# Hi and lo halves of activation tiles interleaved word by word, so that stationary operands have a step of two

## What is computed

```python
# first block: pooling and windowed attention branches, then
ff = square(relu(h2 @ w_up)) @ w_down                 # w_up 1024 x 4096
x = x + rmsnorm(ff)
# second block, layer 0, for latent and for context rows
b_gate, c_gate, u = split(h @ w_in, 3)
y = conv1d_depthwise_3(c_gate * u) + conv_b
h = h + g1 * ((b_gate * y) @ w_out)
h = h + g2 * ((silu(m @ w_gate) * (m @ w_up)) @ w_down)   # hidden 2816
# layer 1: attention whose q and kv come from low-rank latents
q = rms_norm(q_lat) @ w_q_up          # latent 768
kv = rms_norm(kv_lat) @ w_kv_up       # latent 256, keys of both row sets
# then softmax attention, output product, and the same feed-forward (latent rows only)
```

## Time and profile before

| | us |
|---|---|
| median of 3 runs | 1435.29 |
| lowest and highest | 1434.83, 1439.27 |
| the profiled execution | 1439.03 |
| its span, first to last instruction | 1437.2 |

### The profile page before, as it was taken

One profiled execution on the slowest core, in us unless ns is written; L12 is line 12 of the kernel. 1 busy time (PEld: TensorE's weight loads), 2 busy tenths in 40 slices (PEclk: granted clock), 3 DMA queues, 4 the chain that ended last, 5 costly groups with the idle time before them and its releaser, 6 DMA issues.

```text
span 1437.2 us, 17619 instructions
## 1 busy us (share of the span) xinstructions
PE 1342.5 (93%) x7376; PEld 1116.1 (78%) x7376; DVE 803.8 (56%) x1087; ACT 544.6 (38%) x679; POOL 3.5 (0%) x10
## 2 busy tenths in 40 slices
PE   5999779999999999999999999998789988799998
PEld 4877678899777788877777777887667766699997
DVE  5666565458664455662525252537556664656666
ACT  5353343454431123422121212125455552544432
POOL 0000000000000000000000000000000000000000
PEclk9999979999999999999999999999889998899999
DMA  8536436545644532363535353412121311345441
GB/s 307 192 117 251 174 110 249 213 176 180 230 154 197 205 117 88 135 245 127 226 124 227 124 227 125 150 43 92 33 87 48 117 59 59 117 159 194 175 175 59
DMA packets 23782, 218.80 MB, mean 152 GB/s; under 512 B 3104, under 2 KB 8224, under 8 KB 10656
## 3 DMA queue, kind: packets, MB, share of 16 engines
q1 hardware_dynamic: 21328, 209.67, 40.2%
q10 hardware_dynamic: 1520, 4.98, 0.9%
q0 software_dynamic: 864, 3.15, 0.7%
HBM read 216.74 MB, written 1.05 MB: 152 GB/s over the span
## 4 chain that ended last, share of the span: by engine, by line
PE 77%; DVE 12%; ACT 7%; issue 3%; DMA 1%; ACTq 0%; DVEq 0%
PE bank L454 23%; PE bank L455 22%; PE bank L456 22%; DVE w_lo L1432 4%; PE turned L471 3%; PE mod_ps L492 3%; ACT w_hi L980 2%; DVE scaled L1473 2%; PE bank L861 2%; PE small L867 2%; DVE gated L1778 1%; DMA raw<-in_w_branch 1%; ACT xn L987 1%; PE small L511 1%; DMA raw<-in_w_out 1%
## 5 line engine op out<-in xcount | busy, mean ns | idle before, releaser
L454 PE MATMUL bank<-act_hi,w_hi 128*128 128x256 f32 (+1 forms) x1208 | 399.7, 331 | 8.8 <-DVE act_lo L1457 6.3
L455 PE MATMUL bank<-act_lo,w_hi 128*128 128x256 f32 (+1 forms) x1208 | 395.8, 328 | 0.0
L456 PE MATMUL bank<-act_hi,w_lo 128*128 128x256 f32 (+1 forms) x1208 | 395.5, 327 | 0.0
L1432 DVE TENSOR_TENSOR w_lo<-raw,w_hi 128x2048 fp32r<-128x2048 f32 (+4 forms) x168 | 338.2, 2055 | 89.8 <-ACT w_hi L980 89.7
L980 ACT ACTIVATE w_hi<-raw 128x2048 fp32r<-128x2048 f32 (+4 forms) x168 | 280.1, 1715 | 210.0 <-PE bank L456 169.7
L454 PEld LDWEIGHTS bank<-act_hi,w_hi 128*128 128x128 f32 x1208 | 231.8, 192 | 42.8 <-issue 17.0
L455 PEld LDWEIGHTS bank<-act_lo,w_hi 128*128 128x128 f32 x1208 | 232.0, 192 | 19.5 <-issue 0.7
L456 PEld LDWEIGHTS bank<-act_hi,w_lo 128*128 128x128 f32 x1208 | 231.8, 192 | 19.3
L454 PE MATMUL bank<-w_hi,h_hi 128*128 128x512 f32 x392 | 155.4, 396 | 4.0 <-DVE h_lo L1830 2.3
L455 PE MATMUL bank<-w_lo,h_hi 128*128 128x512 f32 x392 | 153.4, 391 | 0.0
L456 PE MATMUL bank<-w_hi,h_lo 128*128 128x512 f32 x392 | 153.3, 391 | 0.0
(11 more groups left out here) (227 smaller groups left out, 1421.5 us busy)
## 6 DMA issues: line engine op xcount, KB each, us to landing
raw<-in_ffn SPq DMA_DIRECT2D x35, 2048.0 KB, 8.1
raw<-in_mlp SPq DMA_DIRECT2D x24, 2048.0 KB, 8.0
raw<-in_mod_gate SPq DMA_DIRECT2D x7, 2048.0 KB, 8.1
raw<-in_conv_in SPq DMA_DIRECT2D x8, 1536.0 KB, 7.1
raw<-in_w_gates SPq DMA_DIRECT2D x4, 2048.0 KB, 8.5
raw<-in_w_branch SPq DMA_DIRECT2D x4, 2048.0 KB, 7.9
raw<-in_mla_q SPq DMA_DIRECT2D x4, 1152.0 KB, 5.3
raw<-in_w_in SPq DMA_DIRECT2D x2, 2048.0 KB, 14.0
```

The lines of the kernel that those rows point to most:

```text
L454: te.matmul(dst, sh, mh, start=(j == 0), stop=False)
L455: te.matmul(dst, sh, ml, start=False, stop=False)
L456: last = te.matmul(dst, sl, mh, start=False, stop=(j == len(terms) - 1))
L1432: ve.tensor_tensor(w_lo[:, s, part], raw[:, at % 2, part], w_hi[:, s, part].bitcast(f32), ALU.subtract).then_inc(lo_ready, 1)
```

## The change

A helper `pair_at` allocates one float32r tile with a last dimension of two and returns two views of it, element 0 as hi and element 1 as lo. The six hi/lo pairs named above are allocated by it, each at the offset where the hi tile stood and over the same bytes as the two together. The views keep their shapes, so the code that writes and reads them is the same: ScalarE writes the high part with a step of two words (8 bytes), VectorE reads it and writes the low part with that step, and TensorE loads 128 columns with it. `act_hi/lo`, `w_hi/lo`, `ypool` and `yattn` stay as they were. The number, kind and order of the instructions of every engine are unchanged.

```diff
+    def pair_at(name, shape, offset):
+
+        both = at(name, shape + [2], offset, f32r)
+        every = (slice(None),) * len(shape)
+        return both[every + (0,)], both[every + (1,)]
...
-    h1_hi = at("h1_hi", [P, 8, SEQ], PH + 8 * K, f32r)
-    h1_lo = at("h1_lo", [P, 8, SEQ], PH + 16 * K, f32r)
+    h1_hi, h1_lo = pair_at("h1_pair", [P, 8, SEQ], PH + 8 * K)
...
-    conv_hi = at("conv_hi", [P, KT, 2, SEQ], PH + 16 * K, f32r)
-    conv_lo = at("conv_lo", [P, KT, 2, SEQ], PH + 32 * K, f32r)
+    conv_hi, conv_lo = pair_at("conv_pair", [P, KT, 2, SEQ], PH + 16 * K)
...
-    h2_hi = at("h2_hi", [P, 4, 2, SEQ], PH + 16 * K, f32r)
-    h2_lo = at("h2_lo", [P, 4, 2, SEQ], PH + 24 * K, f32r)
+    h2_hi, h2_lo = pair_at("h2_pair", [P, 4, 2, SEQ], PH + 16 * K)
...
-    ql_hi = at("ql_hi", [P, QKT, SEQ], PH + 16 * K, f32r)
-    ql_lo = at("ql_lo", [P, QKT, SEQ], PH + 22 * K, f32r)
-    kvl_hi = at("kvl_hi", [P, KVT, KEYS], PH + 28 * K, f32r)
-    kvl_lo = at("kvl_lo", [P, KVT, KEYS], PH + 32 * K, f32r)
+    ql_hi, ql_lo = pair_at("ql_pair", [P, QKT, SEQ], PH + 16 * K)
+    kvl_hi, kvl_lo = pair_at("kvl_pair", [P, KVT, KEYS], PH + 28 * K)
...
-    h3_hi = at("h3_hi", [P, 2, 4, SEQ], PH + 16 * K, f32r)
-    h3_lo = at("h3_lo", [P, 2, 4, SEQ], PH + 24 * K, f32r)
+    h3_hi, h3_lo = pair_at("h3_pair", [P, 2, 4, SEQ], PH + 16 * K)
```

## The result

| | before | after |
|---|---|---|
| median, us (20 runs each) | 1439.53 | 1444.26 |
| lowest and highest, us | 1434.44 and 1441.97 | 1441.14 and 1449.24 |
| profiled execution, us | 1439.03 | 1441.14 |
| its span, us | 1437.2 | 1439.3 |

The ratio of the times is 1.0041, with an interval from 1.003 to 1.0052, so the change costs 5.9 us (4.3 to 7.5 us); the two medians stand 4.7 us apart. The forecast was no change at 1435.3 us with a range up to 1444. The three runs it started from lay low: the kernel before has a median of 1439.5 us over twenty runs, 4.2 us above them.

What follows compares the result with a forecast made beforehand. The prediction took TensorE to set the time, with matmul intervals following the moving columns alone. Its three terms summed 0 + 0 + 0 on the median of the runs, giving 1435.3 us, no change, with a range of 1432 to 1444 us.

Steps and rivals of the forecast that it cites:

- Part 1: TensorE's 1608 weight loads of pair tiles: 0 us taken, 0 to 8 us for a load up to twice as slow.
- rival of a gain: Pairs remove the 13.7 ns excess per 512-column matmul: 20 us saved, 1415 us; chance 0.03.
- The 384-column stream: Query latents' 144 matmuls: 174 ns intervals kept; a load twice as slow would add 50 ns each, 7.2 us.
- rival of the load twice as slow: Stepped loads up to twice as slow, deciding in the query latents' stream alone: up to 8 us, 1443.3 us; chance 0.08.
- Part 2: ScalarE's stepped write of the high part: 632 and 418 ns unchanged, 0 us; doubled per element, 428 ns more per 512 piece.
- Part 3: VectorE's subtraction writing the low part: 692 and 426 ns unchanged, 0 us; doubled per element it would add 532 ns.
- The open places: Six MLP and feed-forward restarts without cover left, where each ns of slower write costs time: 0, or up to 5.8 us.
- a slower engine: ScalarE's and VectorE's stepped access up to twice as slow, at six places and before attention: 8 us, 1443.3 us; chance 0.09.

Runs made afterwards that it cites:

- micro_steps: Computation left out, TensorE streams alone with stationary steps 1 to 8, then ScalarE and VectorE pieces; at 512 columns 227 ns with step 1, 233 with step 2.
- latents_only: The change for the query and key latents alone, against the kernel before: 1440.02 us against 1439.72, ratio 1.0005 (0.9992 to 1.0018).
- micro_shift: Computation left out, TensorE alone, stationary start or both operands shifted; 512 columns, step 1: 226.7 ns unshifted, 233.4 stationary by 16 words, 227.2 both by 32.
- shift_128: Kernel before, no step, with the region of hidden, convolution and latent tiles beginning 128 bytes later: 1447.2 us against 1439.16, ratio 1.0048.

## Why the prediction was wrong

**Part 1 failed, at one sentence.** It said that the interval follows the moving columns alone, and that a load up to twice as slow therefore costs 0 in the 1464 matmuls of 512 columns, because 115 ns of room hide it. The room is real: the floor for a load with step 2 is 118 ns in micro_steps, nearly the 112 the text took for step 1. But room at the end of the load was the wrong thing to look at. The load starts together with the matmul in front of it, and how they are read side by side sets the interval, whether or not the load ends early: at the same 512 columns it was 227 to 234 ns with nothing changed but the place of a contiguous operand, and 230 to 236 with a step of two. Why the two reads act on each other stays open, as said below. The rows it read could not contradict the sentence, since the hidden tiles of the kernel before stand at the place against the moving windows where nothing is lost, a move by 256 bytes keeps it, and the earlier trace rows begin where the intervals after a restart have just settled. The eight intervals ahead of them, and the key latents' stream, both at 231 ns in that very trace, could have: they were not looked at. The term measured +7.56 us in the 512-column streams of the hidden tiles and the convolution and +0.15 in the key latents, 5.7 ns for each of 1320 intervals.

The rows did hold a warning, and the prediction used it in one direction only. Its rival of a gain named the 13.7 ns by which each interval is longer than 512 columns at 2.4 per ns. That excess was taken as something fixed that could only shrink. In the runs it is 13.3 ns in the best place and 16 to 21 in the others.

**The 384-column stream.** Forecast 174 ns, and 215 to 224 ns in the rival of the load twice as slow. It measured 174. The order is the reverse of what the rival said: the short stream, where room was least, pays nothing in this kernel, and the long one pays. That is the place in which it stands; at another place step 2 took 178.5 ns in micro_steps.

**Part 2, ScalarE.** Forecast 632 and 418 ns, measured 666 and 435, at the convolution 698 where it had been 630. The direction was missed; of the bound of 428 ns about 34 came true. Its effect on the time was forecast as 0, and no run tells it from 0: latents_only stands at 1.0005, and the waits of the earlier trace rows went from 4.0 to 3.6 us.

**Part 3, VectorE.** Forecast 692 and 426 ns, measured 693 and 427. Right. The argument by bytes per ns, which gave the same answer for three engines, was right for one of them only, so it can't be called a reason. At a step of four VectorE and ScalarE take 1065 and 1100 ns, for which the argument has no price.

**The open places.** "Each ns of a slower write is a ns of time" was wrong as it stood. At the restart shown above ScalarE's write takes 0.67 us for 0.63, and of the matmuls that run beside it four intervals take (215.82 - 214.88) / 4 = 235 ns instead of 227, so 0.03 us more cover. The stop stays at 0.57 us. Over all six places the wait even shrinks.

**The two pages.** Two hits in a 16-byte line are enough, says the Trainium skill, "SBUF — State Buffer" (Door 1: The DMA port swizzle). VectorE's 693 ns agrees, ScalarE's 658 for 630 and the load's 118 for 112 ns nearly. The rule of adjacent pairs in the Trainium skill, "Vector Engine (DVE) Microarchitecture Reference" (section 5.2), is not borne out at a step of two, where it would have 0.47 us more; at a step of four, 1065 ns are 0.73 ns per element more than 693, of the size it lists. A third page would have spoken for the forecast: the Trainium skill, "TensorE: Matmul & The Clock Gate" (Step-by-step: what each phase is for), says that TensorE has two independent read ports and that loading the next weights doesn't take bandwidth from the running matmul. In micro_shift, where only the relative place of the two operands was changed, the running matmuls of 512 columns came 2 to 8 ns later each, and in shift_128 some 5. So a load is not without effect on them here; whether it is bandwidth that the two share, no run shows.

**The rivals and the number.** The time is nearest to what the rivals of a slower load or a slower engine said (1443.3 us), but neither mechanism is the one that acts: the load's slower rate never decides at step 2, and the slower writes cost nothing that can be told. They were near by accident. The forecast 1435.3 us misses by 9 us, of which 4.2 are the low start of three runs; the rest, 4.7 us, is the term of part 1 (6.6 us in the intervals).

**What stays open.** Shown is that a stationary operand with a step of two costs 6 ns per matmul of 512 columns, by itself and at nearly every place tried (the best was 230 ns); and that for a contiguous one the cost depends on the place of the two reads relative to each other and repeats after 256 bytes. At 384 columns it is there too, but smaller and at fewer of the places tried. That both are one mechanism was only argued: a load with a step passes over addresses at twice the pace of a contiguous one, and so can't keep its place against the moving read. No run tests it. Nor was it studied why the intervals after a pause need some eight matmuls to settle, even at the best place. Which part of the SBUF the two reads share, and whether they share one, was not found, and a moving operand that itself has a step was not tried. No run is clear of noise below the kernel before: it already has the place at which nothing is lost.

## What to carry to other kernels

Where TensorE loads new weights for each matmul of 512 columns, keep the stationary operand contiguous and the distance between the stationary and the moving operand a multiple of 256 bytes; at the other places tried each matmul cost 2 to 8 ns more, and off by 128 bytes it was 0.48% of this kernel. That a load ends early does not mean that it is free: compare the intervals from matmul to matmul, not the length of the load's record and not the waits. And two profiled spans with different mean clocks can hide an effect of this size (2.1 us seen, some 6 true).

## What the runs showed of the hardware

- With an own load before each, matmuls of 256, 320, 384 and 512 columns follow each other every N / 2.4 + 13.3 ns in the best place (119.9, 146.7, 173.3 and 226.7 ns), once settled. At the seven other widths tried from 416 to 508 columns it was 2 to 3 ns more. At 512 columns the other places took 229 to 234 ns. The excess isn't fixed.
- After a pause it takes some eight matmuls of 512 columns, at 224 to 236 ns each, until the interval stands at 227.
- Loads of 128 columns follow one another every 112 ns when contiguous, 118 with a step of two words, 173 with three, 233 with four and 240 to 247 with eight. A step of two costs little in the load's own rate, three and four much.
- A write with a step of two costs ScalarE 4 to 5% and VectorE nothing; with a step of four they take 1.75 and 1.54 times as long.
- A shift of the tiles by 128 bytes, which no instruction count, load record or wait shows, costs 0.48%.
